# Three 256-wide products a tile into one sum, read straight from its bank

## What is computed

```python
# first block
mod = silu(c) @ w_ada + b_ada                     # six vectors of shifts, scales, gates
h = rmsnorm(x) * (1 + sc_a) + sh_a
c_q, c_kv, k_pe, q_g, k_g, v_g, z, b, a, gates = split(h @ w_in)
y_a = mla_branch(...) @ w_o_mla                    # latent attention, 8 heads
y_b = gdn_branch(...) @ w_o_gdn                    # gated delta rule (a recurrence over chunks), 8 heads
x = x + gt_a * ((sigmoid(g_a) * y_a + sigmoid(g_b) * y_b) @ w_o)
h = rmsnorm(x) * (1 + sc_f) + sh_f
x = x + gt_f * ((silu(h @ w_gate) * (h @ w_up)) @ w_down)
x = rmsnorm(x)
# second block
a, gate, q, k, v = split(rmsnorm(x) @ w_in_2)      # conv of width 31, and windowed attention
x = x + rmsnorm(cat(conv_group(a, gate), attention(q, k, v)) @ w_out_2)
x = x + rmsnorm(square(relu(rmsnorm(x) @ w_up_2)) @ w_down_2)
```

## Time and profile before

| | |
|---|---|
| median of 3 runs | 3072.62 us (3068.73 to 3073.01) |
| the profiled execution | 3068.15 us, its span 3066.4 us |
| mean granted TensorE clock | 0.958 |
| TensorE matmul | 2777.1 us (91%), 15408 instructions |
| VectorE | 2141.1 us (70%), 3298 |
| ScalarE | 1345.5 us (44%), 2154 |
| GpSimd | 218.5 us (7%), 198 |
| read from HBM | 560.33 MB, 183 GB/s over the span |

### The profile page before, as it was taken

The page is one execution under the profiler, slowest core; times in us unless marked ns, Lnnn a source line. Parts: engine busy times, 40 slices in busy tenths (PEclk is TensorE's granted clock), DMA queues, the critical chain, the costliest instruction groups (busy, mean ns, idle before and its releaser), DMA issues.

```text
span 3066.4 us, 40448 instructions
## 1 busy us (share of the span) xinstructions
PE 2777.1 (91%) x15408; PEld 2358.6 (77%) x15408; DVE 2141.1 (70%) x3298; ACT 1345.5 (44%) x2154; POOL 218.5 (7%) x198
## 2 busy tenths in 40 slices
PE   1686998989999979999999998999787999999996
PEld 0574776768888868888888887777676888888885
DVE  7867776568778877755565677999757656566665
ACT  1354232254445444444444454344444444444443
POOL 2021000000000200000000062011021000000001
PEclk9997997899999989999999999999898999999998
DMA  8843331147887857755555554444243555555553
GB/s 326 301 152 110 103 113 67 60 161 261 275 279 257 275 181 276 249 192 191 188 191 191 188 185 144 166 153 153 93 151 124 192 187 191 185 186 186 186 186 115
DMA packets 158162, 565.09 MB, mean 184 GB/s; under 512 B 17552, under 2 KB 21776, under 8 KB 157968
## 3 DMA queue, kind: packets, MB, share of 16 engines
q1 hardware_dynamic: 157968, 562.50, 54.8%
HBM read 560.33 MB, written 2.10 MB: 183 GB/s over the span
## 4 chain that ended last, share of the span: by engine, by line
PE 73%; DVE 16%; issue 5%; ACT 2%; POOL 2%; DMA 1%; DVEq 0%; SPq 0%; ACTq 0%; POOLq 0%
PE BK L343 44%; PE BK L344 22%; DVE LO L597 4%; DVE ADA L593 2%; DVE B L804 2%; PE BK L413 1%; DVE B L692 1%; DVE B L593 1%; POOL SQ L840 1%; POOL SQ L851 1%; DVE X L777 1%; DVE B L649 1%; PE BK L385 1%; DMA RAW<-wst_dram 1%; DMA RAW<-wada_dram 1%
## 5 line engine op out<-in xcount | busy, mean ns | idle before, releaser
L343 PE MATMUL BK<-H,HI 128*128 128x512 f32 x6864 | 2465.0, 402 | 127.9 <-DVE LO L597 58.3
L344 PE MATMUL BK<-H,LO 128*128 128x256 f32 x6864 | 1937.7, 282 | 0.0
L343 PEld LDWEIGHTS BK<-H,HI 128*128 128x128 f32 x6864 | 1307.5, 190 | 469.5 <-DVE LO L597 80.8
L489 ACT ACTIVATE HI<-RAW 128x1024 fp32r<-128x1024 f32 x858 | 909.3, 1060 | 1267.6 <-PE BK L344 1211.3
L597 DVE TENSOR_TENSOR LO<-RAW,HI 128x1024 fp32r<-128x1024 f32 x858 | 1054.7, 1230 | 419.5 <-ACT HI L489 418.9
L344 PEld LDWEIGHTS BK<-H,LO 128*128 128x128 f32 x6864 | 1316.3, 192 | 0.2
L840 POOL TENSOR_TENSOR SQ<-SQ,B 128x256 f32<-128x256 f32 x93 | 115.9, 1246 | 1640.3 <-ACT B L512 1634.8
L593 DVE SCALAR_TENSOR_TENSOR ADA<-RAW,SC,ADA 128x1024 f32<-128x1024 f32 x150 | 200.4, 1336 | 11.4 <-DMA RAW<-wada_dram 9.7
L493 ACT ACTIVATE TE<-BK 128x256 f32<-128x256 f32 x492 | 178.7, 367 | 6.7 <-PE BK L344 5.3
L641 DVE TENSOR_TENSOR H<-TV,H 128x256 fp32r<-128x256 f32 x124 | 53.9, 437 | 172.9 <-ACT H L500 172.9
L630 DVE TENSOR_TENSOR TV<-BK,TE 128x256 f32<-128x256 f32 x344 | 143.3, 417 | 43.6 <-ACT TE L493 43.2
(11 more groups left out here) (207 smaller groups left out, 1455.2 us busy)
## 6 DMA issues: line engine op xcount, KB each, us to landing
RAW<-wst_dram SPq DMA_DIRECT2D x858, 512.0 KB, 3.5
RAW<-wada_dram SPq DMA_DIRECT2D x192, 512.0 KB, 4.8
X<-xT_dram SPq DMA_DIRECT2D x8, 512.0 KB, 7.5
B<-bias_dram SPq DMA_DIRECT2D x32, 128.0 KB, 3.3
out_dram<-X SPq DMA_DIRECT2D x4, 512.0 KB, 2.6
CN<-consts_dram SPq DMA_DIRECT2D x1, 968.0 KB, 9.7
CO<-cols_dram SPq DMA_DIRECT2D x1, 308.5 KB, 3.2
B<-pos_dram SPq DMA_DIRECT2D x1, 128.0 KB, 11.4
```

The lines of the kernel that those rows point to most:

```text
L343: e.matmul(bk[:, :], hh, H[:, k, :], start=first, stop=False, skip_group_check=True)
L344: e.matmul(bk[:, 256:512], ll, H[:, k, 0:256], start=False, stop=last, skip_group_check=True).then_inc(S["tile"], 1)
L489: e.activation(HI[:, u % NHL, :], RAW[:, slot, :], ACT.Copy).then_inc(S["hi"], 1)
```

## The change

The tile becomes three 256-wide products into columns 0 to 255 of the bank: high weights times the high half, high weights times the low half, low weights times the high half. The sum is then whole in the bank, and `raw_sum`, `add_sum` and `part_add` go. In their place are `copy_out` (one ScalarE copy from the bank to the goal) and `combine` (one VectorE operation of the bank with another operand, which is the consumer's own first operation where there is one). Activation functions read the bank too. The factor 0.5 that z had got in its addition moves into `gdn_norm`, halved once at the start.

```diff
@@ tensor
-                e.matmul(bk[:, :], hh, H[:, k, :], start=first, stop=False, skip_group_check=True)
-                e.matmul(bk[:, 256:512], ll, H[:, k, 0:256], start=False, stop=last, skip_group_check=True).then_inc(S["tile"], 1)
+                e.matmul(bk[:, 0:256], hh, H[:, k, 0:256], start=first, stop=False, skip_group_check=True)
+                e.matmul(bk[:, 0:256], hh, H[:, k, 256:512], start=False, stop=False, skip_group_check=True)
+                e.matmul(bk[:, 0:256], ll, H[:, k, 0:256], start=False, stop=last, skip_group_check=True).then_inc(S["tile"], 1)
@@ scalar
-            def copy_sum(t, bk, scale, done, free):
+            def copy_sum(dst, bk, done, free):
                 q.wait_ge(done, free)
-                e.activation(t, bk[:, 256:512], ACT.Copy, scale=scale).then_inc(S["ev_a"], 1)
+                e.activation(dst, bk[:, 0:256], ACT.Copy).then_inc(S["ev_a"], 1)
@@ walk
-            def raw_sum(dst, bk, tok, own, free=None, scale=None, part=None):
-                i, t, fr = te.get()
-                a = do("copy_sum", "ev_a", t, bk, 1.0 if scale is None else scale, tok, fr)
-                yield
-                if part is not None:
-                    a = do("part_add", "ev_g", t, part[0], a, part[1])
-                    yield
-                v = do("add_sum", "ev_v", dst, bk, t, scale, a, free)
-                te.release(i, v)
+            def copy_out(dst, bk, tok, own, free=None):
+                a = do("copy_sum", "ev_a", dst, bk, tok, free)
+                own[0].release(own[1], a)
+                return a
+
+            def combine(dst, bk, other, op, tok, own, *free):
+                v = do("tensors", "ev_v", dst, bk[:, 0:256], other, op, tok, list(free))
                 own[0].release(own[1], v)
                 return v
@@ the other half of the first projection (ev_c; ev_kpe, ev_ba and the first heads of ev_qkv alike)
-                    cq_tok[j] = yield from raw_sum(CQ[j], bk, tok, own, x_used, part=half_of(j))
+                    half, hk = half_of(j)
+                    cq_tok[j] = combine(CQ[j], bk, half, add, tok, own, hk, x_used)
+                    yield
@@ plain sums (ev_half, ev_ring, ev_qp, ev_vt, the other heads of ev_qkv, ev_y at ci == 0)
-                    k = yield from raw_sum(t, bk, tok, own, fr)
-                    HD[key] = (i, t, k)
+                    HD[key] = (i, t, copy_out(t, bk, tok, own, fr))
+                    yield
@@ ev_z
-                    k = yield from raw_sum(Z[j], bk, tok, own, v_used1, scale=0.5)
-                    yield
                     i, t, fr = te.get()
-                    a = do("tanh", "ev_a", t, Z[j], 1.0, k, fr)
-                    yield
-                    z_tok[j] = do("scaled", "ev_v", Z[j], t, 1.0, Z[j], add, mult, a)
+                    a = do("tanh", "ev_a", t, bk[:, 0:256], 0.5, tok, fr)
+                    yield
+                    z_tok[j] = do("scaled", "ev_v", Z[j], t, 1.0, bk[:, 0:256], add, mult, a, v_used1)
@@ ev_gate
-                    k = yield from raw_sum(dst[j], bk, tok, own, free2, scale=0.5)
-                    yield
-                    toks[j] = do("tanh", "ev_a", dst[j], dst[j], 1.0, k)
+                    toks[j] = do("tanh", "ev_a", dst[j], bk[:, 0:256], 0.5, tok, free2)
@@ ev_res (ev_ya and ev_yb alike)
-                        i, t, fr = tv.get()
-                        k = yield from raw_sum(t, bk, tok, own, fr)
+                        x_tok[j] = do("scaled", "ev_v", X[:, j, :], bk[:, 0:256], MOD[:, 16 * gate + j:16 * gate + j + 1], X[:, j, :], mult, add,
+                                      tok, [extra, need(mod_tok, 2 * gate + j // 8), x_tok[j]])
+                        own[0].release(own[1], x_tok[j])
                         yield
-                        x_tok[j] = do("scaled", "ev_v", X[:, j, :], t, MOD[:, 16 * gate + j:16 * gate + j + 1], X[:, j, :], mult, add,
-                                      k, [extra, need(mod_tok, 2 * gate + j // 8), x_tok[j]])
-                        tv.release(i, x_tok[j])
@@ up1_outs
                 def e1(bk, tok, own):
+                    c, y, fr = te.get()
+                    a = do("sigmoid", "ev_a", y, bk[:, 0:256], tok, fr)
+                    yield
                     b, t, fr = tv.get()
-                    k = yield from raw_sum(t, bk, tok, own, fr)
-                    yield
-                    c, y, fr = te.get()
-                    a = do("sigmoid", "ev_a", y, t, k, fr)
-                    yield
-                    k = do("tensors", "ev_v", t, t, y, mult, a)
+                    k = combine(t, bk, y, mult, a, own, fr)
                 def e2(bk, tok, own):
-                    b, t, fr = tv.get()
-                    k = yield from raw_sum(t, bk, tok, own, fr)
-                    yield
-                    gb, gt, gk = need(G_, i)
-                    v = do("tensors", "ev_v", t, t, gt, mult, k, gk)
+                    b, t, gk = need(G_, i)
+                    v = combine(t, bk, t, mult, tok, own, gk)
@@ scaled_sum
-                k = yield from raw_sum(dst, bk, tok, own, free)
+                k = combine(dst, bk, R12, mult, tok, own, free, need(r_tok, "r12"))
                 yield
-                return do("tensors", "ev_v", dst, dst, R12, mult, k, need(r_tok, "r12"))
+                return k
@@ ev_y, ci > 0 (up2_outs alike)
-                        k = yield from raw_sum(t, bk, tok, own, fr)
-                        yield
-                        y_tok[j] = do("tensors", "ev_v", Y[j], Y[j], t, add, k, y_tok[j])
+                        y_tok[j] = combine(Y[j], bk, Y[j], add, tok, own, y_tok[j])
```

More of the change, by code:

```diff
@@ L1056, in walk @@
             cw_tok = do("halve", "pre_v", "conv_w", 96, tk_cols)
+            gn_tok = do("halve", "pre_v", "gdn_norm", 1, tk_cols)
             for s in range(X_AT):
@@ L1115, in f @@
                 def f(bk, tok, own):
-                    half_tok[n] = yield from raw_sum(dst, bk, tok, own)
+                    half_tok[n] = copy_out(dst, bk, tok, own)
+                    yield
                 return f
@@ L1179, in ev_kpe @@
             def ev_kpe(bk, tok, own):
-                k = yield from raw_sum(KPE, bk, tok, own, part=half_of(8))
+                half, hk = half_of(8)
+                k = combine(KPE, bk, half, add, tok, own, hk)
+                yield
                 RN["kpe"] = yield from rope(KPE, KPE, k)
@@ L1189, in f @@
                     i, t, fr = tv.get()
-                    k = yield from raw_sum(t, bk, tok, own, fr, part=half_of(9 + j) if j % 8 < 4 else None)
+                    if j % 8 < 4:
+                        half, hk = half_of(9 + j)
+                        k = combine(t, bk, half, add, tok, own, hk, fr)
+                    else:
+                        k = copy_out(t, bk, tok, own, fr)
                     yield
@@ L1199, in ev_ba @@
             def ev_ba(bk, tok, own):
-                lin_tok["ba"] = yield from raw_sum(BA, bk, tok, own, tk_cos, part=half_of(41))
+                half, hk = half_of(41)
+                lin_tok["ba"] = combine(BA, bk, half, add, tok, own, hk, tk_cos)
+                yield
             h_hi = h_tok[8:16]
@@ L1586, in f @@
                 def f(bk, tok, own):
-                    k = yield from raw_sum(Z[j], bk, tok, own, v_used1, scale=0.5)
+                    i, t, fr = te.get()
+                    a = do("tanh", "ev_a", t, bk[:, 0:256], 0.5, tok, fr)
                     yield
-                    i, t, fr = te.get()
-                    a = do("tanh", "ev_a", t, Z[j], 1.0, k, fr)
-                    yield
-                    z_tok[j] = do("scaled", "ev_v", Z[j], t, 1.0, Z[j], add, mult, a)
+                    z_tok[j] = do("scaled", "ev_v", Z[j], t, 1.0, bk[:, 0:256], add, mult, a, v_used1)
                     te.release(i, z_tok[j])
+                    own[0].release(own[1], z_tok[j])
                 return f
@@ L1604, in f @@
                 def f(bk, tok, own):
-                    i, t, fr = tv.get()
-                    k = yield from raw_sum(t, bk, tok, own, fr)
+                    ya_tok[j] = do("scaled", "ev_v", YA[j], YA[j], 1.0, bk[:, 0:256], add, mult, tok, need(ga_tok, j))
+                    own[0].release(own[1], ya_tok[j])
                     yield
-                    ya_tok[j] = do("scaled", "ev_v", YA[j], YA[j], 1.0, t, add, mult, k, need(ga_tok, j))
-                    tv.release(i, ya_tok[j])
                 return f
@@ L1638, in one @@
                     o = B1[:, h, :]
-                    v = do("scaled", "ev_v", o, o, col("gdn_norm"), bk[:, 256 * (h % 2):256 * (h % 2) + 256], mult, mult, m)
+                    v = do("scaled", "ev_v", o, o, col("gdn_norm"), bk[:, 256 * (h % 2):256 * (h % 2) + 256], mult, mult, m, gn_tok)
                     if h % 2:
@@ L1655, in f @@
                     i, t, fr = tv.get()
-                    k = yield from raw_sum(t, bk, tok, own, fr)
```

(16 more changed lines are left out.)

19 lines of the change are left out of this document (4 added, 15 removed).

## The result

The changed kernel takes 3089.36 us (median of 7 runs, 3080.57 to 3092.92) against 3072.62 us before: a ratio of 1.0052, 95% interval 1.0036 to 1.0069. I had forecast 3033 us, faster, with the range ending at 3070: wrong in sign and outside the range. The profiled execution took 3092.92 us, its span is 3091.1 us.

The account below looks back on a forecast made before the run. TensorE, busy 91% of the span, was taken to bound the kernel, with gaps in some stages. Profiled 3068 + 4 (slots) - 43 (way out of the bank) = 3029 us, plus 4 = 3033 as median; range 2980 to 3070.

Parts of the forecast that it names:

- the price of the slots: On TensorE, all 6864 tiles: three 117 ns products instead of a long and a short one, +4 us, bounds -31 and +72.
- The margin of the weight loads: On TensorE: one-column products with a weight load start 106 ns apart, so a 117 ns slot has 11 ns to spare.
- The way out of the bank: Fewer ScalarE copies, VectorE and GpSimd additions shorten stages where TensorE has gaps: 43 us saved in sum, nothing in wide stages.
- first half: First projection, 86 to 173 us: fewer bank waits, but weights are awaited too; 3 us saved, bounds 0 and 12.
- second half: First projection, 173 to 322 us: the way through GpSimd goes, the VectorE operation stays; 6 us saved, bounds 0 and 17.
- queries and keys with the recurrence: Stretch 322 to 467 us: 12 blocks lose an addition in VectorE's queue between the recurrence's steps; 3 us saved.
- latent attention: Stretch 467 to 662 us: 28 blocks lose an addition, and some bank waits go; 7 us saved, bounds 0 and 12.
- the ends of chains: Last sums before residual norms and the kernel's end: a copy and an addition leave, 0.8 us four times, 3 us saved.
- rival (c): Weight loads hold every slot to 120 ns or more: +29 us, 3097 profiled, median 3101; decided at 118.6 ns; chance 0.11.
- The clock: From 173 to 662 us, shorter gaps give back a little of the 1.2 GHz time: 4 us saved, bounds 0 and 20.
- Rival (a): From 173 to 662 us, freed places only lengthen waits for the recurrence: savings about 20 us, median 3056; chance 0.16.
- (b): Gaps shrink more than taken, through upper bounds and the clock: 85 us saved, 2987 profiled, median 2991; chance 0.13.

Follow-up runs that it names:

- e3_ladder: Kernel after, with products of other widths and weight columns in stretches of 128 tiles; only start distances read: 120.0 ns at 256 columns, 226.7 at 512.
- e1_split: Kernel before, old way out of the bank kept, only the 512-wide product cut into two 256-wide ones: 3124.83 us, ratio 1.0171.
- e4_ladder2: Kernel after, with other widths, weight columns and operand rows in 21 stretches; only start distances read: 113.3 ns at 256 columns with 64 weight columns.

## Why the prediction was wrong
**The step that failed** is the price of the slots. I read the two slots of the earlier trace rows, 0.23 and 0.12 us, as prices by width, found one twice the other, and concluded that a matmul has no price of its own. Two things in the same rows spoke against it. At the full clock of 2.4 GHz, which the stretches show, 512 and 256 columns take 213 and 107 ns, so 16 to 22 and 10 ns were left over, which my reading (117 / 256 = 0.457 ns a column) only renamed; and where products of two widths alternate, the distances of two starts say what a pair takes, not what each takes. The pair is what can be used: 346 to 352 ns for 320 ns of columns, 26 to 32 ns over for two products. Three products then take 320 + 3 x 13 to 16 = 359 to 368 ns, and the sum is +65 us or more with every tile exposed, not +4. The ladder later gave 13.3 ns a product at 256 and at 512 columns, measured with equal neighbours. In the fast stretch, two of those account for the old tile (320 + 26.7 = 346.7, which is what its starts show); the 6 ns more of the slow stretch stay open. The margin of the weight loads was misread as well. In the earlier trace rows I divided 1.70 us by 16, but in the trace the first two of those starts are 26 ns apart and the others 111 to 112, so a slot of 117 ns had 5 ns to spare and not 11.

**The terms of the sum.** Slots: +4 us predicted; +52.5 us by the medians of `e1_split`, +61.2 by its profiled span. It is less than 6864 x 10.5 = 72 mainly because stages with gaps hide their part (above: 1.9 us paid of 16). The way out of the bank: 43 us predicted, 35.5 by medians, 36.5 by profiled spans. The difference of the two kernels' spans closes: 3066.4 + 61.2 - 36.5 = 3091.1. By stage, kernel after against `e1_split`, from the starts of the tiles: first half 4.4 us shorter (I took 3), second half 11.5 (6), queries and keys with the recurrence 2.7 longer (3 shorter), latent attention 5.8 (7), convolution 2.8 (4), windowed attention 6.5 (6). Output of the recurrence and `w_o` gained 7.7, for which I had only the ends of chains; 2160 to 2400, for which I had 5, gained none. In the wide stages the two kernels differ by some 1 us or less each.

**The bounds and the rivals.** The upper bound of the slot, 120 ns and +72 us, stood in the text, and rival (c) with its 3097 was 4 us off the profiled 3093, and a slot of 120 ns on the far side of its deciding point, 118.6, did make the kernel slower. That closeness is partly luck: its +72 was 11 us too much by the spans and its -43 was 6 too much, and the two errors mostly cancel. Still, I gave it 0.11 and left it out of the range, because the short slots in both stretches "read alike" at 117. Its mechanism is not what the runs show: loads that can't catch up would set a floor, which a wide product covers, while the price is there at 384 and 512 columns too. Of the fixed price of a matmul in the Trainium skill (TensorE: Matmul & The Clock Gate, Back-to-back issue gap), which I set aside for the rows: its direction was right, its figure of 2.5 ns, and so the 17 us, too small for fp32r by the ladder's 13.3. Otherwise most things went as said: of the 43.8 us that tiles waited for VectorE's addition, 18.4 are left, 11.6 for ScalarE's copy and 6.8 for merged operations; VectorE has 469 operations less, though each freed 0.37 us of busy time and not 0.42 (1969 us in all, where I wrote 1945), and ScalarE 398, 0.28 us each; the weight loads are 22272; and the wide stages got longer, which I had named as the sign that the slot is wrong. The clock did not do as forecast in the latent attention: 0.84 before and after, and 0.79 to 0.81 in the stage from 173. Rival (a) is wrong in size, since the way out brought 36 us and not 20, but right about the recurrence: from 322 to 662 us of the kernel before only 3 of my 10 us came. In (b) I added 15 us for the clock where the bound above it is 20; it changes nothing, as (b) lay on the wrong side.

## What to carry to other kernels
Cutting a product in two costs its fixed price wherever TensorE is full: at the full clock 12 to 16 ns with fp32r operands here, 2.5 ns with two-byte ones, and nothing at 1.2 GHz. Price it from the columns at the granted clock and the length of a whole repeating group, never from the distance between two starts of unlike products. A cheaper evacuation paid here only in stages where TensorE has gaps, and there it can carry a dearer product. So choose the form of a tile by stage, not for the kernel as a whole.

## What the runs showed of the hardware that I had not expected
- An fp32r matmul with a load of 128 weight columns takes its columns at 2.4 GHz plus 13.3 ns at 256, 320, 384 and 512 columns, 12.0 at 272, 11.7 at 288 and 16.0 at 448; a bf16 one plus 2.5 ns. At a granted clock of 0.50 an fp32r one of 256 columns takes 213.3 ns, its columns at 1.2 GHz and nothing more.
- TensorE can be busy without a pause and be granted 1.2 GHz. In `e3_ladder`, three products of 128 columns each, one behind the other:

```profile
1180.00:1230.00 50.00, 50.00 (x237) 50.00 (x236) 0.50 0.48 159
```

The clock is 0.50 over the whole stretch and the starts are 213.3 ns apart. Before it TensorE ran products of 256 columns and then these, some 112 ns apart, at the full clock and without a pause. With 64 weight columns the same width kept the clock at 1.00, with starts some 60 ns apart. Products of 256 columns on only 32 rows, in `e4_ladder2`, fell to 1.2 GHz too, from starts 120 ns apart to 213.3.
